# A hybrid decoder layer on one core: where the recurrence's masked matrices are transposed

## Chip, cores and metric

One core of a Trainium2 chip. The metric is the device time of one execution, in microseconds (us). The kernel before takes 2487.46 us (median of three runs, 2486.31 to 2492.12).

## The reference

One layer of a decoder is computed for a prompt of 1024 tokens and for 8 x 4 sample tokens: normalisation, one wide projection, differential attention (4 heads) beside an RWKV-7 group (8 heads of size 64), an output projection, a gated convolutional feed-forward part and a per-layer embedding. The change lies in the RWKV-7 recurrence of the prompt:

```
def _wkv_scan(s0, r, w, k, v, kk, a):
    def step(s, inp):
        r_t, w_t, k_t, v_t, kk_t, a_t = inp
        sa = jnp.einsum('bhvk,bhk->bhv', s, -kk_t)
        s = (s * w_t[:, :, None, :] + sa[..., None] * (kk_t * a_t)[:, :, None, :]
             + v_t[..., None] * k_t[:, :, None, :])
        return s, jnp.einsum('bhvk,bhk->bhv', s, r_t)
```

The kernel doesn't step through the tokens. It cuts the prompt into 16 chunks of 64 tokens. For each chunk and head it forms the chunk's transition, for which a unit triangular 64 x 64 matrix must be inverted; a short scan over the 16 chunks follows.

## The kernel before

The program is a row of blocks, each with its own instruction list for every engine; the engines wait for one another by semaphores. The block of the change is `rwkv_transitions` (L1150). Its successor is `rwkv_scan` (L1433), and then come the attention, the output projection and the rest.

`rwkv_transitions` takes the chunks two at a time, called b = 0 and b = 1, in 8 turns; the first is written out, the other seven are a loop. The 8 heads lie as 4 pairs, two heads in the 128 partitions. A tile of 128 x 512 holds, for 4 pairs, a 128 x 128 matrix that is block diagonal with two blocks of 64 x 64.

The order of the work is that of the program text on each engine. A turn is, on TensorE: products that form the triangular matrices (L1272), 32 transposes of the pair blocks (L1283), then six levels, then the last products (L1320 to L1334). The inversion goes by levels: at level n the blocks of size 2^n along the diagonal are joined to blocks of size 2^(n+1). A level has four steps for each of b = 0 and b = 1:

- mask: VectorE multiplies the current matrix (at level 0 `za` in SBUF, later the product `q0` in PSUM) by the level's mask `levbd` into `ut` (L1367); what remains lies within the blocks of size 2^(n+1), that is, up to level 4 within blocks of 32 x 32 on the diagonal
- transpose: TensorE transposes the four 128 x 128 matrices of `ut` into PSUM, `q1` (L1292)
- copy: VectorE copies `q1` to `ubd` in SBUF (L1373)
- product: TensorE multiplies with `ubd` as weights into `q0` (L1304)

On each engine both chunks' instructions of one step stand before those of the next: mask b0, mask b1, copy b0, copy b1 on VectorE; transposes of b0 and b1, products of b0 and b1 on TensorE. ScalarE copies the product to `wz` for the next level (L1391), after the next level's mask has read it. At level 0, TensorE has another group of matmuls behind the products (L1312), which needs `vs` from GpSimd (L1240). `q1` also holds, at the start of a turn, what VectorE reads into `m2` and `m4` (L1355, L1356); the semaphore `m4` keeps the transposes of level 0 from writing `q1` before. GpSimd fills `bd` for the next turn (L1225) while the levels run.

Of the kernel before, what the change touches and what calls it, by code (L numbers as in the profile page):

```python
# [904 lines left out]
NLEV = 6  # L905
# [244 lines left out]
def rwkv_transitions(kit, a, NR, BK, V, Y):  # L1150
# [14 lines left out]
    nc = kit.nc  # L1165
# [4 lines left out]
    with ExitStack() as ctx:  # L1170
# [87 lines left out]
        @block.tensor  # L1258
        def _(pe):
            pe.wait_ge(S["const_in"], 16 * len(consts))  # L1260
            mm = nc.tensor.matmul

            def turn(i, first):
                for b in range(2):
                    c = i * 2 + b
                    pe.wait_ge(S["placed"], c * 8 + 8)
                    for q, dst, freed, sem in ((0, q0, ("phi_kept", "r_kept"), "p1"), (1, q1, ("z_kept", "y_kept"), "p2")):
                        if not first:
                            for name in freed:
                                pe.wait_ge(S[name], c - 1)  # L1270
                        for p in range(NPAIR):
                            last = mm(dst[b][:, p, :], bd[:, b, q, p, :], NR[:, p, :, ds(c * C, C)],  # L1272
                                      start=True, stop=True)
                        last.then_inc(S[sem], 1)
                for r, (qa, qb) in enumerate(((0, 1), (2, 3))):
                    for b in range(2):
                        for n, (q, dst) in enumerate(((qa, q2), (qb, q3))):
                            if r == 1:
                                pe.wait_ge(S["kept"], i * 8 + 2 * b + n + 1)
                            elif not first:  # L1280
                                pe.wait_ge(S["a2v_kept" if n == 0 else "xbd"], i * 2 - 1 + b)
                            for p in range(NPAIR):
                                last = nc.tensor.transpose(dst[b][:, p, :], bd[:, b, q, p, :], ident[:])  # L1283
                            last.then_inc(S["turn"], 1)
                for lev in range(NLEV):
                    for b in range(2):
                        n = (i * NLEV + lev) * 2 + b
                        pe.wait_ge(S["ut"], n + 1)
                        if lev == 0:
                            pe.wait_ge(S["m4"], i * 2 + b + 1)  # L1290
                        for p in range(NPAIR):
                            last = nc.tensor.transpose(q1[b][:, p, :], ut[:, b, p, :], ident[:])  # L1292
                        last.then_inc(S["uturn"], 1)
                    for b in range(2):
                        n = (i * NLEV + lev) * 2 + b
                        pe.wait_ge(S["ubd"], n + 1)
                        if lev == 0:
                            pe.wait_ge(S["m3"], i * 2 + b + 1)
                            pe.wait_ge(S["adi"], i * 2 + b + 1)
                        else:  # L1300
                            pe.wait_ge(S["wz"], (i * (NLEV - 1) + lev - 1) * 2 + b + 1)
                        src, w = za if lev == 0 else wz, C if lev == NLEV - 1 else 2 * C
                        for p in range(NPAIR):
                            last = mm(q0[b][:, p, 0:w], ubd[:, b, p, :], side(src[:, b, p])[:, 0:w], start=True, stop=True)  # L1304
                        last.then_inc(S["made"], 1)
                    if lev == 0:
                        for b in range(2):
                            pe.wait_ge(S["m2"], i * 2 + b + 1)
                            pe.wait_ge(S["stacked"], i * 6 + b * 3 + 2)
                            pe.wait_ge(S["kept"], i * 8 + 8)  # L1310
                            for p in range(NPAIR):
                                last = mm(q2[b][:, p, 0:C], m2[:, b, p, :], vs[:, b, p, :], start=True, stop=True)  # L1312
                            last.then_inc(S["a2v"], 1)
                for b in range(2):
                    c = i * 2 + b
                    pe.wait_ge(S["wbd"], c + 1)
                    pe.wait_ge(S["a2v_kept"], c + 1)
                    pe.wait_ge(S["stacked"], i * 6 + b * 3 + 3)
                    for p in range(NPAIR):
                        last = mm(q3[b][:, p, :], wbd[:, b, p, :], side(na[:, b, p]), start=True, stop=True)  # L1320
                    last.then_inc(S["tx"], 1)
                for b in range(2):
                    c = i * 2 + b
                    pe.wait_ge(S["tn_kept"], c + 1)
                    for p in range(NPAIR):
                        last = mm(q0[b][:, p, :], tn[:, b, p, :], side(bm[:, b, p]), start=True, stop=True)
                    last.then_inc(S["pr"], 1)
                    pe.wait_ge(S["xst"], c + 1)
                    pe.wait_ge(S["xbd"], c + 1)
                    for p in range(NPAIR):  # L1330
                        mm(q1[b][:, p, 0:C], turned[:, b, 0, p, :], xst[:, b, p, :], start=True, stop=False)
                        mm(q1[b][:, p, 0:C], turned[:, b, 1, p, :], vs[:, b, p, :], start=False, stop=True)
                        mm(q1[b][:, p, C:P], xbd[:, b, p, :], bm[:, b, p, 1, :], start=True, stop=False)
                        last = mm(q1[b][:, p, C:P], turned[:, b, 2, p, :], m4[:, b, p, :], start=False, stop=True)  # L1334
                    last.then_inc(S["zy"], 1)
            turns(pe, turn)

        @block.vector
        def _(dve):
# [3 lines left out]
            def turn(i, first):  # L1343
                for b in range(2):
                    c = i * 2 + b
                    dve.wait_ge(S["p1"], c + 1)
                    if not first:
                        dve.wait_ge(S["zy"], c - 1)
                    tt(za[:, b, :, 1], q0[b][:, :, 0:C], pairs(below[:]), ALU.mult)\
                        .then_inc(S["adi0"], 1)  # L1350
                    tt(bm[:, b, :, 1], q0[b][:, :, C:P], pairs(incl[:]), ALU.mult).then_inc(S["m3"], 1)
                for b in range(2):
                    c = i * 2 + b
                    dve.wait_ge(S["p2"], c + 1)
                    tt(blocks(m2[:, b]), spread(q1[b][:, :, 0:C]), pairs(strict[:]), ALU.mult).then_inc(S["m2"], 1)  # L1355
                    tt(m4[:, b], q1[b][:, :, C:P], pairs(incl[:]), ALU.mult).then_inc(S["m4"], 1)  # L1356
                for lev in range(NLEV):
                    for b in range(2):
                        n = (i * NLEV + lev) * 2 + b
                        if lev == 0:  # L1360
                            dve.wait_ge(S["adi"], i * 2 + b + 1)
                        else:
                            dve.wait_ge(S["made"], n - 1)
                        if not (first and lev == 0):
                            dve.wait_ge(S["uturn"], n - 1)
                        z = za[:, b, :, 1] if lev == 0 else q0[b][:, :, C:P]
                        tt(blocks(ut[:, b]), spread(z), pairs(levbd[:, lev]), ALU.mult).then_inc(S["ut"], 1)  # L1367
                    for b in range(2):
                        n = (i * NLEV + lev) * 2 + b
                        dve.wait_ge(S["uturn"], n + 1)  # L1370
                        if not (first and lev == 0):
                            dve.wait_ge(S["made"], n - 1)
                        nc.vector.tensor_copy(ubd[:, b], q1[b][:]).then_inc(S["ubd"], 1)  # L1373
                for b in range(2):
                    c = i * 2 + b
                    dve.wait_ge(S["tx"], c + 1)
                    tt(blocks(tn[:, b]), spread(q3[b][:, :, 0:C]), pairs(pairbd[:]), ALU.mult).then_inc(S["tn_kept"], 1)
                for b in range(2):
                    c = i * 2 + b
                    here = ds(c * C, C)  # L1380
                    dve.wait_ge(S["pr"], c + 1)
                    tt(BK[:, 0, :, here], q0[b][:, :, 0:C], pairs(eye[:]), ALU.add).then_inc(S["phi_kept"], 1)
                    tt(NR[:, :, 1, here], q0[b][:, :, C:P], NR[:, :, 1, here], ALU.add).then_inc(S["r_kept"], 1)
# [1463 lines left out]
```

## Time and profile before

| what | value |
|---|---|
| median of three runs | 2487.46 us |
| the profiled execution | 2489.03 us |
| its span, first to last instruction | 2487.3 us |
| mean granted TensorE clock | 0.879 |
| TensorE busy, whole span | 2007.8 us (81%) |
| VectorE busy | 1218.6 us (49%) |
| ScalarE busy | 833.5 us (34%) |
| GpSimd busy | 450.6 us (18%) |

In the rows, PE is TensorE's matmuls, PEld its loading of weights, DVE is VectorE, ACT ScalarE, POOL GpSimd. Times count from the first instruction. A matmul's end is modelled. A row of the timeline merges instructions of one line that follow each other; what stands in brackets at its end is the idle time of the engine before it, and what ended it. A product of 32-bit matrices is two matmul instructions for each pair, so the 8 products of a step, 4 pairs of two chunks, are 16; a transpose is one.

### The profile page before, as it was taken

What the parts mean: (1) busy time and instruction counts of PE and PEld (TensorE: products, weight loads), DVE (VectorE), ACT (ScalarE), POOL (GpSimd) and SP (SyncE); (2) the same over time, 40 slices, a digit from 0 to 9 for tenths busy, and PEclk for the clock granted to TensorE, in tenths of its full rate; (3) what the DMA queues carried; (4) which work ended last, traced back from release to release, by engine and by line L of the source; (5) the groups of instructions that cost most, each with busy time, mean ns of one, the idle gap of its engine ahead of it and who ended that gap; (6) DMA issues with size and microseconds to landing.
All of it is one profiled execution on the core that took longest, in us unless ns stands there. A gap on an engine that the chain in (4) does not pass through costs nothing. (4 is left out here: it accounts for less than half of the span.)

```text
span 2487.3 us, 35830 instructions
## 1 busy us (share of the span) xinstructions
PE 2007.8 (81%) x13340; PEld 1908.8 (77%) x13340; DVE 1218.6 (49%) x1996; ACT 833.5 (34%) x1408; POOL 450.6 (18%) x606
## 2 busy tenths in 40 slices
PE   1999972439999993664565568999999998999997
PEld 1999971328889893554344568999999998999997
DVE  5001106635455523765662157656555556445475
ACT  3111114213343322553000145433333334434454
POOL 0000001443232210001960202211111110011022
PEclk8999995769999965877666689999999999999998
DMA  2222213010000005224862054111111113454443
GB/s 99 89 94 87 102 71 126 35 44 1 0 0 0 0 0 116 51 52 112 290 203 91 35 203 143 64 43 44 51 43 52 43 52 121 134 169 161 138 129 120
DMA packets 75720, 211.89 MB, mean 85 GB/s; under 512 B 11506, under 2 KB 17570, under 8 KB 75314
## 3 DMA queue, kind: packets, MB, share of 16 engines
q1 hardware_dynamic: 55986, 156.30, 20.3%
q0 software_dynamic: 8224, 31.81, 3.4%
q10 hardware_dynamic: 11392, 22.20, 2.8%
q8 instruction: 75, 1.23, 0.2%
q14 instruction: 43, 0.35, 0.0%
HBM read 179.04 MB, written 31.24 MB: 85 GB/s over the span
## 5 line engine op out<-in xcount | busy, mean ns | idle before, releaser
L2018 PE MATMUL bh_acc<-Mh,bh_wh 128*128 128x352 f32 x2016 | 659.5, 327 | 33.9 <-DVE bh_wl L2288 28.3
L2018 PE MATMUL bh_acc<-Ml,bh_wh 128*128 128x352 f32 x2016 | 652.6, 324 | 0.0
L2018 PE MATMUL bh_acc<-Mh,bh_wl 128*128 128x352 f32 x2016 | 652.5, 324 | 0.0
L2018 PEld LDWEIGHTS bh_acc<-Mh,bh_wh 128*128 128x128 f32 x2016 | 383.4, 190 | 36.7 <-DVE bh_wl L2288 29.7
L2018 PEld LDWEIGHTS bh_acc<-Ml,bh_wh 128*128 128x128 f32 x2016 | 384.3, 191 | 0.0
L2018 PEld LDWEIGHTS bh_acc<-Mh,bh_wl 128*128 128x128 f32 x2016 | 383.1, 190 | 0.0
L2288 DVE TENSOR_TENSOR bh_wl<-bh_raw,bh_wh 128x1024 fp32r<-128x1024 f32 x170 | 201.2, 1184 | 167.3 <-ACT bh_wh L2093 167.2
L403 PE MATMUL in_acc<-Hh,in_wh 128*128 128x352 f32 x624 | 202.5, 324 | 24.5 <-DVE in_wl L386 24.5
L2093 ACT ACTIVATE bh_wh<-bh_raw 128x1024 fp32r<-128x1024 f32 x170 | 173.9, 1024 | 116.4 <-PE bh_acc L2018 106.4
L403 PE MATMUL in_acc<-Hl,in_wh 128*128 128x352 f32 x624 | 201.1, 322 | 0.0
L403 PE MATMUL in_acc<-Hh,in_wl 128*128 128x352 f32 x624 | 200.9, 322 | 0.0
L2328 DVE TENSOR_TENSOR cv_u<-bh_acc,ffn_r 128x352 f32<-128x352 f32 x132 | 67.8, 514 | 191.9 <-PE bh_acc L2018 189.9
L386 DVE TENSOR_TENSOR in_wl<-in_raw,in_wh 128x1024 fp32r<-128x1024 f32 x26 | 31.8, 1225 | 252.1 <-ACT in_wh L374 252.1
L403 PEld LDWEIGHTS in_acc<-Hh,in_wh 128*128 128x128 f32 x624 | 118.0, 189 | 24.6 <-DVE in_wl L386 24.6
L532 PE MATMUL ap_sc<-ap_kh,ap_qs 128*128 128x512 f32 (+3 forms) x96 | 45.0, 470 | 93.3 <-DVE ap_kl L588 48.8
L403 PEld LDWEIGHTS in_acc<-Hl,in_wh 128*128 128x128 f32 x624 | 118.1, 189 | 0.0
L403 PEld LDWEIGHTS in_acc<-Hh,in_wl 128*128 128x128 f32 x624 | 117.8, 189 | 0.0
L288 ACT ACTIVATE in_out<-in_acc 128x1056 f32<-128x1056 f32 x26 | 27.4, 1055 | 251.9 <-PE in_acc L403 251.9
L2137 ACT ACTIVATE cv_v<-cv_u,par 128x352 f32<-128x352 f32 (+1 forms) x66 | 45.3, 686 | 175.5 <-DVE cv_u L2328 77.0
L532 PEld LDWEIGHTS ap_sc<-ap_kh,ap_qs 128*128 128x128 f32 x96 | 22.9, 239 | 99.3 <-issue 49.4
L2137 ACT ACTIVATE cv_g<-cv_u,par 128x352 f32<-128x352 f32 (+1 forms) x66 | 45.3, 686 | 119.7 <-DVE cv_u L2328 73.7
L1304 PE MATMUL rt_q<-rt_wz,rt_ubd 128*128 128x128 f32 (+1 forms) x640 | 81.5, 280 | 4.1 <-DVE rt_ubd L1373 3.4
(334 smaller groups left out, 3417.2 us busy)
## 6 DMA issues: line engine op xcount, KB each, us to landing
bh_raw<-dram_w_down SPq DMA_DIRECT2D x48, 512.0 KB, 3.7
bh_raw<-dram_w_up SPq DMA_DIRECT2D x44, 512.0 KB, 3.6
as_vp<-dram_v_pool ACTq DMA_DIRECT2D x64, 256.0 KB, 3.3
as_kT<-dram_k_pool SPq DMA_DIRECT2D x64, 256.0 KB, 4.0
dram_projT<-in_out POOLq DMA_DIRECT2D x26, 528.0 KB, 3.0
in_raw<-dram_w_in SPq DMA_DIRECT2D x26, 512.0 KB, 3.6
bh_raw<-dram_w_o SPq DMA_DIRECT2D x24, 512.0 KB, 3.7
bh_raw<-dram_w_gate SPq DMA_DIRECT2D x24, 512.0 KB, 3.6
```

Of the source, the lines that this page charges most:

```text
L288: self.nc.scalar.activation(self.out[:, b], self.acc[:, b, :, 0:self.parts[0][1]], ACT.Copy).then_inc(self.drained, 1)
L386: nc.vector.tensor_tensor(wl[:, buf], raw[:, buf], wh[:, buf].bitcast(F32), ALU.subtract).then_inc(residued, 1)
L403: last = nc.tensor.matmul(acc[:, b, n, 0:size], w[:, buf, k, :], x[:, u * kt + k, at:at + size], start=(u == 0 and k == 0 and q == 0), sto ...
L532: last = nc.tensor.matmul(sc[:, c, at:at + n], qs[:, hb, c, i * P:(i + 1) * P], k[:, hb, c, at:at + n], start=(k is kh), stop=(k is kl and ...
L1304: last = mm(q0[b][:, p, 0:w], ubd[:, b, p, :], side(src[:, b, p])[:, 0:w], start=True, stop=True)
L2018: ins = mm(out, w(k), x, start=first and k == 0 and q == 0, stop=last and k == len(xs) - 1 and q == 2)
L2093: nc.scalar.activation(whs[b][:, 0:n], raws[b][:, 0:n], ACT.Copy).then_inc(rounded, 1)
L2137: nc.scalar.activation(conv_of(m, t), u[m % 2][:, cols(t)], ACT.Identity, bias=tap("cb", m), scale=tap("cw0", m)).then_inc(tap0, 1)
L2288: nc.vector.tensor_tensor(wls[b][:, 0:n], raws[b][:, 0:n], whs[b][:, 0:n].bitcast(F32), ALU.subtract).then_inc(residued, 1)
L2328: ins = nc.vector.tensor_tensor(z[:, 2 + at:2 + at + w], src[:, 0:w], R1[:, at:at + w], ALU.mult)
```

## The change

At levels 0 to 4 VectorE transposes `ut` straight into `ubd`, both in SBUF, by its block transpose, one instruction of 128 x 512 for each chunk. It turns every block of 32 x 32 in its place, which is the transpose of the whole where all that isn't zero lies in 32 x 32 blocks on the diagonal. Level 5, whose blocks are 64 x 64, keeps the transpose on TensorE and the copy. The waits follow: the product waits for `ubd` as before, a mask waits for the transpose that read its buffer, and TensorE's wait for `m4` moves to level 5.

```diff
                 for lev in range(NLEV):
-                    for b in range(2):
+                    for b in range(2 if lev == NLEV - 1 else 0):
                         n = (i * NLEV + lev) * 2 + b
                         pe.wait_ge(S["ut"], n + 1)
-                        if lev == 0:
-                            pe.wait_ge(S["m4"], i * 2 + b + 1)
+                        pe.wait_ge(S["m4"], i * 2 + b + 1)
                         for p in range(NPAIR):
                             last = nc.tensor.transpose(q1[b][:, p, :], ut[:, b, p, :], ident[:])
                         last.then_inc(S["uturn"], 1)
...
-                        if not (first and lev == 0):
-                            dve.wait_ge(S["uturn"], n - 1)
+                        if lev:
+                            dve.wait_ge(S["ubd"], n - 1)
+                        elif not first:
+                            dve.wait_ge(S["uturn"], i * 2 - 1 + b)
                         z = za[:, b, :, 1] if lev == 0 else q0[b][:, :, C:P]
                         tt(blocks(ut[:, b]), spread(z), pairs(levbd[:, lev]), ALU.mult).then_inc(S["ut"], 1)
                     for b in range(2):
                         n = (i * NLEV + lev) * 2 + b
-                        dve.wait_ge(S["uturn"], n + 1)
                         if not (first and lev == 0):
                             dve.wait_ge(S["made"], n - 1)
-                        nc.vector.tensor_copy(ubd[:, b], q1[b][:]).then_inc(S["ubd"], 1)
+                        if lev < NLEV - 1:
+                            dve.wait_ge(S["ut"], n + 1)
+                            nc.vector.transpose(ubd[:, b].rearrange("p a c -> p (a c)"),
+                                                ut[:, b].rearrange("p a c -> p (a c)")).then_inc(S["ubd"], 1)
+                        else:
+                            dve.wait_ge(S["uturn"], i * 2 + b + 1)
+                            nc.vector.tensor_copy(ubd[:, b], q1[b][:]).then_inc(S["ubd"], 1)
```

## Rows read from the trace of the kernel before

**Rows 1.** Chain of waits, its earliest piece: start us, us, what.

```profile
1446.52 1.06 ACT bh_wh L2093
```

**Rows 2.** Stretches, all engines: PE, PEld, DVE, ACT, POOL busy; clock; DMA share; GB/s.

```profile
640.00:680.00 40.00, 38.11 (x315) 35.12 (x314) 22.27 (x38) 14.99 (x32) 12.01 (x24) 1.00 0.00 0
```

**Rows 3.** Timeline, start of two turns: start us, us, engine, line, operation, tiles.

```profile
640.25 0.42 DVE L1349 TENSOR_TENSOR rt_za<-rt_q,rt_below 128x256 f32<-128x256 f32 x1 [3.69 <-PE rt_q L1272]
...
681.12 0.42 DVE L1349 TENSOR_TENSOR rt_za<-rt_q,rt_below 128x256 f32<-128x256 f32 x1 [3.69 <-PE rt_q L1272]
```

**Rows 4.** Timeline, one steady level (level 3) of that turn.

```profile
657.32 0.69 DVE L1367 TENSOR_TENSOR rt_ut<-rt_q,rt_levbd 128x512 f32<-128x512 f32 x1 [0.49 <-PE rt_q L1304]
658.04 0.60 ACT L1391 ACTIVATE rt_wz<-rt_q 128x512 f32<-128x512 f32 x1 [2.03 <-DVE rt_ut L1367]
...
658.07 0.66 PE L1292 MATMUL rt_q<-rt_ident,rt_ut 128*128 128x128 f32 x4
658.21 0.69 DVE L1367 TENSOR_TENSOR rt_ut<-rt_q,rt_levbd 128x512 f32<-128x512 f32 x1 [0.20 <-PE rt_q L1304]
658.82 0.68 DVE L1373 COPY rt_ubd<-rt_q 128x512 f32<-128x512 f32 x1
...
658.96 0.66 PE L1292 MATMUL rt_q<-rt_ident,rt_ut 128*128 128x128 f32 x4 [0.23 <-DVE rt_ut L1367]
...
659.64 2.05 PE L1304 MATMUL rt_q<-rt_wz,rt_ubd 128*128 128x128 f32 x16
...
660.83 0.69 DVE L1367 TENSOR_TENSOR rt_ut<-rt_q,rt_levbd 128x512 f32<-128x512 f32 x1 [0.49 <-PE rt_q L1304]
```

**Rows 5.** Timeline, levels 0 and 1 of the same turn.

```profile
642.64 3.66 PE L1283 MATMUL rt_q<-rt_ident,rt_bd 128*128 128x128 f32 x32
...
644.48 1.44 DVE L1367 TENSOR_TENSOR rt_ut<-rt_za,rt_levbd 128x512 f32<-128x512 f32 x2
...
646.13 1.04 PE L1292 MATMUL rt_q<-rt_ident,rt_ut 128*128 128x128 f32 x8
...
646.77 1.29 DVE L1373 COPY rt_ubd<-rt_q 128x512 f32<-128x512 f32 x2 [0.85 <-PE rt_q L1292]
...
647.51 2.05 PE L1304 MATMUL rt_q<-rt_za,rt_ubd 128*128 128x128 f32 x16 [0.35 <-DVE rt_ubd L1373]
648.05 0.73 POOL L1240 TENSOR_TENSOR rt_vs<-rt_turned 128x256 f32<-128x256 f32 x1
...
649.40 1.90 PE L1312 MATMUL rt_q<-rt_vs,rt_m 128*128 128x64 f32 x16
...
651.13 1.05 PE L1292 MATMUL rt_q<-rt_ident,rt_ut 128*128 128x128 f32 x8
...
651.78 1.29 DVE L1373 COPY rt_ubd<-rt_q 128x512 f32<-128x512 f32 x2 [1.49 <-PE rt_q L1292]
...
652.61 2.05 PE L1304 MATMUL rt_q<-rt_wz,rt_ubd 128*128 128x128 f32 x16 [0.43 <-DVE rt_ubd L1373]
```

**Rows 6.** Groups of VectorE by shape: busy us, mean ns, idle before.

```profile
L2288 DVE TENSOR_TENSOR bh_wl<-bh_raw,bh_wh 128x1024 fp32r<-128x1024 f32 x146 | 178.2, 1221 | 122.8 <-ACT bh_wh L2093 122.7
L1373 DVE COPY rt_ubd<-rt_q 128x512 f32<-128x512 f32 x96 | 64.5, 686 | 23.5 <-PE rt_q L1292 22.3
...
L614 DVE SCALAR_TENSOR_TENSOR ap_wgt<-ap_pexp,ap_small,ap_wgt 128x512 f32<-128x512 f32 x4 | 3.0, 752 | 0.4
...
L610 DVE TENSOR_SCALAR ap_wgt<-ap_pexp,ap_small 128x512 f32<-128x512 f32 x4 | 1.9, 476 | 0.0
```

**Rows 7.** Stretches in the attention: PE busy (count), clock, DMA share, GB/s.

```profile
1003.70:1007.10 3.40, 1.50 (x12) 1.00 0.00 0
...
1007.00:1008.00 1.00, 1.00 (x6) 0.58 0.00 0
...
1010.60:1017.40 6.80, 3.38 (x31) 1.00 0.00 0
```

**Rows 8.** A stretch in the scan, columns as in rows 2.

```profile
890.00:900.00 10.00, 10.00 (x49) 10.00 (x48) 3.22 (x8) 2.48 (x6) 2.20 (x6) 0.50 0.01 2
```

## Prediction

> **What bounds the kernel now.** I read the chain of waits first. Its earliest piece stands at 1446.52 us [rows 1], so it says nothing of the transitions, which run from about 555 to 885 us. The stretches come next: in 640 to 680 us TensorE is busy 38.11 of 40 us, VectorE 22.27, ScalarE 14.99, with the granted clock at 1.00 and no DMA [rows 2]. That looks like a stage bound by TensorE, but these times include the modelled tails of matmuls, so only the timeline tells who waits for whom. The two starts of L1349, one turn apart, give a turn of 681.12 - 640.25 = 40.87 us [rows 3], and there are eight turns: 16 chunks by two, and L1373's 96 copies are 8 x 6 levels x 2 chunks [rows 6].
>
> A steady level first [rows 4]. b0 and b1 are the two chunks. The masking of b0 (ut, L1367) starts at 657.32 and that of b1 at 658.21, since b1's waits for its own product. TensorE transposes b0 from 658.07 for 0.66 us, while VectorE masks b1. The copy of b0 (L1373) starts at 658.82, 0.61 after b1's masking started, which is the pitch of 512-column operations on VectorE standing behind one another; it has no idle time before it. So b0's transposes are hidden behind the masking of b1. The product (L1304) starts at 659.64, 0.14 after that copy ends, and the next masking at 660.83, another 1.19 later. A level is 660.83 - 657.32 = 3.51 us, bound by a ring through VectorE and TensorE: masking of b1 0.61, copy 0.68 and 0.14, product to next masking 1.19, masking of b0 to that of b1 0.89.
>
> The first two levels of a turn are different [rows 5]. In level 0 VectorE has masked both chunks by 645.92, but TensorE still works through the 32 transposes of the pair blocks (L1283, 642.64 for 3.66 us). It reaches the transposes of ut only at 646.13, and the copies start at 646.77 after 0.85 us of idle time. In level 1 it is worse: TensorE has 16 matmuls of L1312 queued ahead (649.40 for 1.90), the transposes start at 651.13, and VectorE waits 1.49 us until 651.78. Here the transposes on TensorE, which executes in order, end last.
>
> **The change part by part.** Removed at levels 0 to 4: 8 transposes on TensorE per level (1.04 to 1.05 us where they stand together, two lots of 0.66 in a steady level), their semaphores, and 2 PSUM copies per level. Added: 2 VectorE transposes, SBUF to SBUF, 128x512, in the place of the copies, in the same order (mask b0, mask b1, transpose b0, transpose b1). VectorE has the same number of instructions. Its wait for TensorE becomes a wait for its own masking, which has ended when the transpose's turn comes: b0's masking ends 0.20 us before b1's starts, and b1's ends while b0 is transposed. Nothing else is queued behind it that was not behind the copy. Level 5 and the rest of the turn stay.
>
> *The duration T of a VectorE transpose.* No row shows one. The copy that it replaces takes 0.686 mean, but reads PSUM. The nearest SBUF rows of 512 columns are 0.476 (L610, one tensor input) and 0.752 (L614, two) [rows 6]; level 0's two maskings, from SBUF, take 1.44 together. Below, 0.476. Above, twice the elements: 1.22 (L2288, 1024 columns), if 4-byte elements go through in two passes. I take 0.71, between the copy and L614, since a transpose is one pass with some filling ahead of the first output.
>
> *Steady levels (2 to 4).* The ring is unchanged except for T in place of 0.68, so a level costs T - 0.68 = 0.03 more and the three of them lose 0.09 us. TensorE's transposes were hidden there, and taking them out gives nothing back.
>
> *Level 0.* The transpose of b0 starts at VectorE's pitch, about 645.85, ends at 646.56, and the product starts 0.05 later (the gap after the copy there), at 646.61 in place of 647.51: 0.90 earlier. TensorE has finished L1283 by 646.30.
>
> *Level 1.* Two things may end last. TensorE: L1312 follows the start of the product by 649.40 - 647.51 = 1.89, and the next instruction came 651.13 - 649.40 = 1.73 after that, so it is free at 646.61 + 3.62 = 650.23. What L1312 needs from GpSimd for b1 (the vs of 648.05, 0.73 long [rows 5]) is there at 648.78, before b1's half at about 649.4. VectorE: 646.61 + 1.19 + 0.89 + 0.61 + 0.71 + 0.14 = 650.15. So TensorE by a hair: the product starts at 650.23 in place of 652.61, 2.38 earlier (0.90 of it from level 0).
>
> *Sum.* 2.38 - 0.09 = 2.29 us per turn, 8 turns, 18.3 us. The turns follow one another through the same rings, and the scan starts after the stage, with next to no DMA beside it [rows 2, 8], so all of it should arrive at the end. The profiled execution took 2489.03 (span 2487.3, and 1.7 around it): 2470.7. The median of the three runs is 1.57 lower, so I forecast 2469.
>
> In general the gain of a turn is the smaller of 3.09 - T and 3.88 - 2T, less 3(T - 0.68). At 0.476 that is 3.2 us, 25.8 in all, 2462.
>
> *A figure of the Trainium skill weighed against this.* The rows put the gain where TensorE's transposes are late, in levels 0 and 1, and at nothing where they are hidden [rows 4, 5]. The Trainium skill, page "VectorE: DVE Perf Modes", section "The three transpose paths", lists 390 ns for a 128x128 bf16 transpose on TensorE and 311 ns on VectorE. By that difference, as an estimate, the 8 x 5 x 8 = 320 tiles would save 0.079 each wherever they stand, 25 us and 2462; that is rival D. I go by the rows.
>
> **The rivals.**
>
> *A: the transpose is slow.* At T over 0.96 also b1's product waits, since its transpose then ends more than 0.89 after b0's. The five levels then lose T - 0.96 each on top, and the gain of a turn is about 10.7 - 10T: nothing at T = 1.07, and at 1.22 a loss of 1.5 per turn, 12 us, 2499. For it: 4-byte data, and no row of this operation. Against it: the rows of 512 columns lie between 0.476 and 0.752 [rows 6]. The Trainium skill, "Vector Engine (DVE) Microarchitecture Reference", section 3.8, has the transpose array sustain one element per cycle and lane, which speaks against two passes; no row here shows it.
>
> *B: the clock falls, the case on the other side of the forecast.* The place is the bursts of levels 1 to 4. TensorE is left with 2.05 us of matmuls per 3.51 us, where it had two lots of transposes of 0.66 besides [rows 4]. If that drops the clock from 2.4 to 1.2 GHz, the four bursts of levels 2 to 5 take 2.05 longer each, 8.2 per turn against 2.3 gained: 47 us, 2534. It decides from 1.1 slow bursts per turn on. For it: in the scan TensorE's records fill 10 of 10 us and the clock stays at 0.50 [rows 8], and in 3.40 us from 1003.70 TensorE was busy 1.50 and the clock fell right after [rows 7]. Against it: in 6.80 us from 1010.60 it was busy 3.38, and the clock stayed at 1.00 [rows 7]; the levels after the change stand nearer to this one, though for longer. The Trainium skill, "TensorE: Matmul & The Clock Gate", part 4, says that transposes on TensorE don't count as its being busy; by that rule these levels hold the clock on the matmuls alone already, and taking the transposes out changes nothing. No run here separates the two.
>
> *C: the transposes at level 0 or 1 are hidden anyway* by something that I overlook, for instance GpSimd's adds, which use SBUF while the transposes run (the last vs at 648.05 [rows 5]), or a wait in front of L1312. Then only about half the gain remains: 1.2 per turn, 2478.
>
> *D: VectorE's transpose is the quicker one in every level*, as the rate of L610 would make it: with T at 0.476 a steady level loses 0.20 too, 3.2 us per turn, 2462 as above. No row of a transpose bears it out.
>
> **How the numbers follow.** Forecast (T between 0.6 and 0.8, 2.0 to 2.7 per turn) 0.73; its own range is 2464 to 2474, with some two microseconds on either side for the spread of the runs (2486.31 to 2492.12). A 0.10, B 0.07, C 0.05, D 0.05. The measurement tells about 0.3%, 7.5 us. Faster: forecast, C, D and some of neither, 0.82. Same: A with T between 0.9 and 1.1, and a part of C, 0.07. Slower: A at 1.2, and B, 0.11. The range 2460 to 2481 takes in C and D and leaves out A's long end and B.
>
> **What would show it.** Steady levels still 3.5 us apart, with the transpose 0.61 behind the second masking and TensorE idle some 1.3 us between bursts; the idle times of 0.85 and 1.49 before VectorE's second pair gone in levels 0 and 1; L1312 followed at once by level 1's product; a turn of about 38.6 us; clock 1.00 throughout. The forecast is wrong if a VectorE transpose takes over 0.9, if the product waits for ScalarE's wz (it ends at 658.64 for b0, 0.9 ahead of need [rows 4]), or if the turn shrinks by steady levels.

## The result, and the profile after

| | before | after |
|---|---|---|
| median of the runs | 2487.42 us (4 runs, 2486.31 to 2492.12) | 2471.34 us (4 runs, 2467.08 to 2474.39) |
| ratio after to before, 95% | | 0.9931 (0.9911 to 0.9951) |
| profiled execution, its span | 2489.03, 2487.3 | 2467.08, 2464.9 |
| turn, start of `za` to the next one | 40.87 | 38.52 |
| stage: first `za` to the scan's first memset | 329.00 | 309.95 |

The kernel is faster by 0.5 to 0.9%, which is 12 to 22 us; 2469 was forecast, and the median is 2.3 above that. The lines have moved: masks are now L1368, the VectorE transpose L1375, the copy of level 5 L1379, the product L1303, TensorE's own transposes L1291, and the group behind level 0 L1311.

The turn comes from the timeline of VectorE (start us, busy us, engine, line, operation, tiles), two starts of `za` in the kernel after. They answer to [rows 3]:

```profile
637.53 0.42 DVE L1348 TENSOR_TENSOR rt_za<-rt_q,rt_below 128x256 f32<-128x256 f32 x1 [3.69 <-PE rt_q L1272]
...
676.05 0.42 DVE L1348 TENSOR_TENSOR rt_za<-rt_q,rt_below 128x256 f32<-128x256 f32 x1 [3.69 <-PE rt_q L1272]
```

The stage's two ends, from the same view:

```profile
559.64 0.42 DVE L1348 TENSOR_TENSOR rt_za<-rt_q,rt_below 128x256 f32<-128x256 f32 x1 [17.09 <-PE rt_q L1272]
...
869.59 0.27 DVE L1520 MEMSET rn_states<- 128x256 f32 x1 [4.64 <-PEq L71]
```

The stretch of [rows 2], by engine, in the kernel after (PE, PEld, DVE, ACT and POOL busy, clock, DMA share, GB/s):

```profile
640.00:680.00 40.00, 34.89 (x296) 33.23 (x295) 23.39 (x42) 16.48 (x36) 12.60 (x26) 1.00 0.00 0
```

TensorE is less busy, the others a little more, since 40 us now hold more of a turn. The clock stays at 1.00, which is 2.4 GHz.

The price that no row of before had, the VectorE transpose, from the groups of VectorE's work by shape (count, then busy us and mean ns, then idle time before):

```profile
L1375 DVE STREAM_TRANSPOSE rt_ubd<-rt_ut 128x512 f32<-128x512 f32 x80 | 51.8, 684 | 0.0
...
L1379 DVE COPY rt_ubd<-rt_q 128x512 f32<-128x512 f32 x16 | 11.1, 692 | 1.6 <-PE rt_q L1291 1.6
```

684 ns, as much as the copy that it replaces (686 in [rows 6], 692 for the ones left at level 5), and VectorE never sat idle in front of one.

Levels 0 and 1 of that turn, from the timeline of all engines; they answer to [rows 5]:

```profile
639.92 3.66 PE L1283 MATMUL rt_q<-rt_ident,rt_bd 128*128 128x128 f32 x32
...
641.76 1.44 DVE L1368 TENSOR_TENSOR rt_ut<-rt_za,rt_levbd 128x512 f32<-128x512 f32 x2
643.12 1.29 DVE L1375 STREAM_TRANSPOSE rt_ubd<-rt_ut 128x512 f32<-128x512 f32 x2
...
643.88 2.05 PE L1303 MATMUL rt_q<-rt_za,rt_ubd 128*128 128x128 f32 x16 [0.30 <-DVE rt_ubd L1375]
...
645.76 1.90 PE L1311 MATMUL rt_q<-rt_vs,rt_m 128*128 128x64 f32 x16
...
646.57 1.29 DVE L1375 STREAM_TRANSPOSE rt_ubd<-rt_ut 128x512 f32<-128x512 f32 x2
...
647.50 2.00 PE L1303 MATMUL rt_q<-rt_wz,rt_ubd 128*128 128x128 f32 x16
```

The idle times of 0.85 and 1.49 in front of VectorE's second pair are gone. From the first mask to level 1's product it takes 647.50 - 641.76 = 5.74; before it took 652.61 - 644.48 = 8.13 [rows 5]. Level 1's product follows L1311 with no idle time: TensorE is the one that ends last there.

A steady level, from the same view; it answers to [rows 4]:

```profile
652.18 0.69 DVE L1368 TENSOR_TENSOR rt_ut<-rt_q,rt_levbd 128x512 f32<-128x512 f32 x1 [0.74 <-PE rt_q L1303]
...
652.90 0.60 ACT L1397 ACTIVATE rt_wz<-rt_q 128x512 f32<-128x512 f32 x1 [2.04 <-DVE rt_ut L1368]
653.07 0.69 DVE L1368 TENSOR_TENSOR rt_ut<-rt_q,rt_levbd 128x512 f32<-128x512 f32 x1 [0.20 <-PE rt_q L1303]
...
653.68 1.29 DVE L1375 STREAM_TRANSPOSE rt_ubd<-rt_ut 128x512 f32<-128x512 f32 x2
...
654.52 2.05 PE L1303 MATMUL rt_q<-rt_wz,rt_ubd 128*128 128x128 f32 x16 [1.49 <-ACT rt_wz L1397]
655.72 0.69 DVE L1368 TENSOR_TENSOR rt_ut<-rt_q,rt_levbd 128x512 f32<-128x512 f32 x1 [0.74 <-PE rt_q L1303]
```

A level takes 655.72 - 652.18 = 3.54, where it took 3.51. The releaser that the product's row names, ScalarE's `wz`, is not the one: for b0 it had ended at 652.90 + 0.60 = 653.50, while the transpose of b0, started at 653.68, ends 0.68 later, 0.16 before the product. Where a row names an engine that had long been done, look for the other input of the waiting instruction.

### The profile page after: what moved, and what is told of

Read it like the earlier page. It is cut to its first block and busy times, and to the rows that moved or that the text cites. A ratio compares the mean times of both kernels' runs of the same rounds, so it can differ in the third digit from the quotient of the medians.

```text
span 2464.9 us, 35120 instructions
## 1 busy us (share of the span) xinstructions
PE 1957.7 (79%) x13020; PEld 1868.9 (76%) x13020; DVE 1215.9 (49%) x1996; ACT 833.1 (34%) x1408; POOL 450.4 (18%) x606
## 5 line engine op out<-in xcount | busy, mean ns | idle before, releaser
L532 PE MATMUL ap_sc<-ap_kh,ap_qs 128*128 128x512 f32 (+3 forms) x96 | 43.1, 449 | 98.1 <-DVE ap_kl L588 49.5
L1303 PE MATMUL rt_q<-rt_wz,rt_ubd 128*128 128x128 f32 (+1 forms) x640 | 81.1, 280 | 35.8 <-ACT rt_wz L1397 31.3
L1303 PEld LDWEIGHTS rt_q<-rt_wz,rt_ubd 128*128 128x128 f32 x640 | 74.5, 192 | 42.1 <-ACT rt_wz L1397 37.1
```

The costliest lines, as they stand in the source:

```text
L532: last = nc.tensor.matmul(sc[:, c, at:at + n], qs[:, hb, c, i * P:(i + 1) * P], k[:, hb, c, at:at + n], start=(k is kh), stop=(k is kl and ...
```

## Experiments

Seven kernels ran. In the table the time is the median (one run where no spread stands), the ratio is to the kernel before in the same study (medians 2486.48 for experiments 1 to 4, 2486.83 for 5 to 7), and `turn`, `level` (a steady one, start to start) and `stage` are from each one's trace. Experiments 1 to 4 ran on one chip, 5 to 7 on another. Line numbers shift by a few from one experiment to the next; the tiles tell which step a row is.

| | us | ratio, 95% | turn | level | stage |
|---|---|---|---|---|---|
| before | 2487.42 | 1 | 40.87 | 3.51 | 329.00 |
| after | 2471.34 | 0.9931 (0.9911 to 0.9951) | 38.52 | 3.54 | 309.95 |
| 1: levels 0, 1 only | 2475.36 (2470.67 to 2478.84) | 0.9952 (0.9935 to 0.9969) | 38.44 | 3.51 | 309.55 |
| 2: levels 2 to 4 only | 2494.08 (2491.2 to 2501.33) | 1.003 (1.0007 to 1.0052) | 40.95 | 3.54 | 329.69 |
| 3: other order | 2457.49 (2456.23 to 2459.01) | 0.9886 (0.987 to 0.9903) | 36.74 | 2.77 | 296.41 |
| 4: transposes twice | 2524.6 | | 44.24 to 46.94 | 4.41 to 5.9 | 366.83 |
| 5: 4, with TensorE transposes | 2505.02 | | 43.01 | 4.41 | 345.57 |
| 6: 4, with TensorE products | 2502.62 | | 43.01 | 4.41 | 345.81 |
| 7: 3, L1311 spread | 2448.05 (2446.52 to 2452.93) | 0.984 (0.9815 to 0.9864) | 35.77 | 2.76 | 288.47 |

### 1 and 2: which levels give the gain

Experiment 1 leaves levels 2 to 4 to TensorE and the copy, experiment 2 leaves levels 0 and 1 to them. The waits follow (not shown).

```diff
-                    for b in range(2 if lev == NLEV - 1 else 0):
+                    for b in range(2 if lev in PEL else 0):
...
-                        if lev < NLEV - 1:
+                        if lev not in PEL:
                             dve.wait_ge(S["ut"], n + 1)
# experiment 1: PEL = (2, 3, 4, 5); experiment 2: PEL = (0, 1, 5)
```

> VectorE's transpose at levels 0 and 1 alone; levels 2 to 5 transpose on TensorE and copy, as before. Theory (the gain comes where TensorE's in-order queue delayed the transposes, in levels 0 and 1): the turn falls from 40.88 to about 38.5 us, as with the whole change (38.52), steady levels at 3.51, some 2468 to 2472. Rival (each tile taken off TensorE is worth the same, wherever it stands): two fifths of the gain of 2.36 per turn, a turn of about 39.9 us, some 2480.

> The other part: VectorE's transpose at levels 2, 3 and 4 alone. Theory: TensorE's transposes are hidden there behind the second masking, so nothing is gained: a turn of 40.9 to 41.0 us, steady levels 3.53, time within 0.2% of before. Rival: three fifths of the gain, a turn of about 39.5 us, some 2476.

Two turns' starts of experiment 1, from VectorE's timeline, then of experiment 2:

```profile
641.26 0.42 DVE L1350 TENSOR_TENSOR rt_za<-rt_q,rt_below 128x256 f32<-128x256 f32 x1 [3.69 <-PE rt_q L1273]
...
679.70 0.42 DVE L1350 TENSOR_TENSOR rt_za<-rt_q,rt_below 128x256 f32<-128x256 f32 x1 [3.69 <-PE rt_q L1273]
```

```profile
639.16 0.42 DVE L1350 TENSOR_TENSOR rt_za<-rt_q,rt_below 128x256 f32<-128x256 f32 x1 [3.69 <-PE rt_q L1273]
...
680.11 0.42 DVE L1350 TENSOR_TENSOR rt_za<-rt_q,rt_below 128x256 f32<-128x256 f32 x1 [3.69 <-PE rt_q L1273]
```

Levels 0 and 1 alone give the whole gain and a little more (40.87 - 38.44 = 2.43 a turn, against 2.35 with all five levels), and the three steady levels alone lose 0.08. Both turns are as the theory had them; an edge in every level, which asked for turns of 39.9 and 39.5, is refuted by both.

The times of the whole program are not as the theory had them. Experiment 1 was to take 2468 to 2472 and took 2475.36; experiment 2 was to stay within 0.2% of before and is slower by 0.1 to 0.5%. Experiment 1 gained 11 us where its stage gained 329.00 - 309.55 = 19.45, and experiment 2 lost 7.6 where its stage lost 0.7. The other kernels lean the same way: for the one after the change and for experiments 1, 2, 3 and 7, the median lies 1.8 to 8.3 us above what the median before and the change of the stage together would give. What lies outside the stage, which no experiment touched, also differs between the profiled executions: the stage begins between 556.09 and 563.31 us, and from its end to the end of the span it takes 1595.3 to 1603.3. For experiment 1 these were 563.31 and 1602.4, where before had 557.48 and 1600.8: 5.8 and 1.6 later, the 7.4 between its span's gain of 12.0 and its stage's gain. For experiment 2 the profiled execution, the fastest of the seven, doesn't show where the 7.6 of the median lie. The cause of these differences stays open; they don't follow the levels, since levels 2 to 4 on VectorE go with a median 4.0 us lower between experiment 1 and the whole change, and 7.6 higher between before and experiment 2. So the gain of this change is best read from the stage, and the median carries some microseconds that the stage doesn't explain.

### 3: the order on VectorE

With the transpose on VectorE, its order need not be that of the kernel before. Here b0 is transposed before b1 is masked, at levels 0 to 4. The bodies of the two loops over b, unchanged, become functions that are not shown: `mask`, and `swap`, which transposes or, at level 5, copies.

```diff
+                    order = (mask, 0), (mask, 1), (swap, 0), (swap, 1)
+                    if lev < NLEV - 1:
+                        order = (mask, 0), (swap, 0), (mask, 1), (swap, 1)
+                    for step, b in order:
+                        step(lev, b)
```

> The whole change with VectorE's order at levels 0 to 4 made mask b0, transpose b0, mask b1, transpose b1 (before: both masks, then both transposes). Theory (a steady level is a ring in which b0's transpose stands behind the masking of b1): the ring opens, and VectorE's own work with the wait for its mask's end (0.69 and some 0.15, then 0.61, for each chunk) sets a level of about 2.9 us in place of 3.53. From level 0's product to level 1's stays 3.6, set by TensorE. A turn of about 36.3 us, 2.2 less than with the change, some 2453. Rival (the ring is set by product, ScalarE's copy wz and semaphores, and VectorE's order doesn't matter): 38.5 us. Rival (the wait for its own mask costs VectorE more than is won): levels of 3.5 us or more.

Experiment 3, timeline of all engines, a steady level:

```profile
647.31 0.69 DVE L1367 TENSOR_TENSOR rt_ut<-rt_q,rt_levbd 128x512 f32<-128x512 f32 x1
...
648.03 0.71 DVE L1375 STREAM_TRANSPOSE rt_ubd<-rt_ut 128x512 f32<-128x512 f32 x1
648.67 0.65 DVE L1367 TENSOR_TENSOR rt_ut<-rt_q,rt_levbd 128x512 f32<-128x512 f32 x1
...
648.89 1.15 PE L1303 MATMUL rt_q<-rt_wz,rt_ubd 128*128 128x128 f32 x8 [0.30 <-DVE rt_ubd L1375]
649.36 0.71 DVE L1375 STREAM_TRANSPOSE rt_ubd<-rt_ut 128x512 f32<-128x512 f32 x1
...
650.08 0.69 DVE L1367 TENSOR_TENSOR rt_ut<-rt_q,rt_levbd 128x512 f32<-128x512 f32 x1
```

A level is 2.77, a little under the 2.9 that was expected. VectorE has no idle time in front of any of its rows, and its four operations start 0.72, 0.64, 0.69 and 0.72 apart. Yet it is not VectorE's own pace that closes the level, as the expectation had it: the last distance, from b1's transpose to the next mask of b0, is longer than the 0.64 from b0's transpose to b1's mask, and that next mask stands 650.08 - 648.89 = 1.19 behind b0's product, the same distance as in a steady level before [rows 4]. So b0's own ring ends last: mask to transpose 0.72, transpose to product 0.86, product to mask 1.19, 2.77 in all. With 0.64 in place of the last 0.72, VectorE alone would need 2.69, an estimate that no run tests. A transpose follows its own mask by 0.69 to 0.72, where a transpose behind the other chunk's mask stands 0.61 after it (653.07 to 653.68 above): waiting for the operation just before costs some 0.1, less than was allowed for.

Level 0 fell short. Its rows in experiment 3:

```profile
639.20 1.15 PE L1303 MATMUL rt_q<-rt_za,rt_ubd 128*128 128x128 f32 x8
...
640.69 1.13 PE L1303 MATMUL rt_q<-rt_za,rt_ubd 128*128 128x128 f32 x8 [0.35 <-DVE rt_ubd L1375]
...
641.66 1.90 PE L1311 MATMUL rt_q<-rt_vs,rt_m 128*128 128x64 f32 x16
...
643.39 2.00 PE L1303 MATMUL rt_q<-rt_wz,rt_ubd 128*128 128x128 f32 x16
```

b1's product comes 1.49 after b0's, the 16 matmuls of L1311 stand behind it on TensorE, and so they start 2.46 after b0's product, where it was 1.88. Level 1's product waits for those 16, not for its `ubd`: 4.19 from product to product where 3.6 was expected. That makes the turn 36.74 in place of 36.3. The kernel is faster than the one after the change all the same, by 2471.34 - 2457.49 = 13.9 us, and by 309.95 - 296.41 = 13.5 in the stage.

### 4: a transpose of double length

Each VectorE transpose runs twice, the first time into `spare`, a new tile that nothing reads.

```diff
+                            nc.vector.transpose(spare[:, b].rearrange("p a c -> p (a c)"),
+                                                ut[:, b].rearrange("p a c -> p (a c)"))
                             nc.vector.transpose(ubd[:, b].rearrange("p a c -> p (a c)"),
                                                 ut[:, b].rearrange("p a c -> p (a c)")).then_inc(S["ubd"], 1)
```

> The whole change with each of VectorE's transposes at levels 0 to 4 made twice, the first time into a tile that nobody reads. Theory (the transpose is on the ring, and b1's product follows b1's transpose once this ends over 0.89 us after b0's): each level loses 0.61 for the added transpose ahead of b0's product and 0.33 since the products then stand 1.22 apart in place of 0.89; five levels, 4.7 per turn: 43.2 us, a steady level near 4.5, some 2508. Rival (VectorE has idle time in the level that takes it): 38.5 us.

The turns are 1 to 4 us longer than the longer ring alone was to make them. TensorE's timeline in experiment 4, products of three levels one after the other, shows the first 4.41 apart and the next 5.33:

```profile
662.49 2.33 PE L1303 MATMUL rt_q<-rt_wz,rt_ubd 128*128 128x128 f32 x16 [0.35 <-DVE rt_ubd L1377]
...
666.90 3.25 PE L1303 MATMUL rt_q<-rt_wz,rt_ubd 128*128 128x128 f32 x16 [2.08 <-DVE rt_ubd L1377]
...
672.23 3.78 PE L1303 MATMUL rt_q<-rt_wz,rt_ubd 128*128 128x128 f32 x16 [2.08 <-DVE rt_ubd L1377]
```

and the stretches of the same kernel show what goes with it (length, TensorE busy, granted clock, DMA share, GB/s):

```profile
660.00:664.00 4.00, 3.63 (x31) 1.00 0.00 0
664.00:668.00 4.00, 1.92 (x15) 0.94 0.00 0
668.00:672.00 4.00, 2.14 (x11) 0.50 0.00 0
672.00:676.00 4.00, 3.77 (x16) 0.50 0.00 0
676.00:680.00 4.00, 1.92 (x10) 0.50 0.00 0
680.00:684.00 4.00, 3.62 (x26) 0.85 0.00 0
```

TensorE works 2.33 and idles 2.08 in each level, and inside the levels the clock drops from 2.4 to 1.2 GHz. The same products then take 3.25 to 3.78 in place of 2.33. The kernel after idles 1.49 per level and holds the clock. The expectation had only the longer ring: 43.2 and 2508.

### 5 and 6: does a transpose on TensorE hold the clock?

Both are experiment 4 with extra work on TensorE behind the products of levels 1 to 3, the stretch in which it would idle: 8 transposes of the identity in experiment 5, 4 products of identity by identity (8 matmul instructions) in experiment 6. Nothing reads their results.

```diff
+                    if lev in (1, 2, 3):
...
+                        for b in range(2):
+                            for p in range(NPAIR):
+                                nc.tensor.transpose(q1[b][:, p, :], ident[:], ident[:])
# experiment 6, in place of the last three lines:
+                        for p in range(NPAIR):
+                            mm(q1[p % 2][:, p, :], ident[:], ident[:], start=True, stop=True)
```

> The kernel with each transpose on VectorE made twice, and on TensorE, behind the products of levels 1, 2 and 3, eight transposes of the identity that nobody reads (0.9 us in an idle time of 2.08). Theory (in the run without them the turn was 45.8 in place of 43.2 us because the clock fell to 0.50 in the longer idle times, and TensorE's transposes count as activity, as they did before the change): the clock stays at 1.00, steady levels of 4.41, a turn of 43.1 us. The Trainium skill's rule (transposes on TensorE do not count as its being busy; page TensorE: Matmul & The Clock Gate, part 4): the clock falls as without them, and the turn stays near 45.8 us. Rival (the fall has nothing to do with the idle times): 45.8 us as well, here and with matmuls in their place.

> The same with four products of the identity with itself (eight matmul instructions of 128 columns) in place of the eight transposes. Theory, and the rule of the page as well: the clock stays at 1.00, steady levels of 4.41, a turn of 43.1 us. Rival (idle times don't matter): the clock falls and the turn is near 45.8 us.

Experiment 5, TensorE's timeline:

```profile
655.45 2.33 PE L1303 MATMUL rt_q<-rt_wz,rt_ubd 128*128 128x128 f32 x16 [0.35 <-DVE rt_ubd L1383]
657.62 1.04 PE L1310 MATMUL rt_q<-rt_ident 128*128 128x128 f32 x8
659.86 2.33 PE L1303 MATMUL rt_q<-rt_wz,rt_ubd 128*128 128x128 f32 x16 [1.21 <-DVE rt_ubd L1383]
```

and the stretch of 620 to 680 us in experiments 4, 5 and 6, in that order:

```profile
620.00:680.00 60.00, 47.04 (x321) 0.81 0.00 1
```

```profile
620.00:680.00 60.00, 51.50 (x414) 1.00 0.00 0
```

```profile
620.00:680.00 60.00, 51.60 (x415) 1.00 0.00 0
```

Added work made the program faster than experiment 4, by 19.6 and 22.0 us between single runs on two chips, on which the kernel before agrees to 0.4 us (2486.48 and 2486.83): the idle time per level falls from 2.08 to 1.21, the clock stays at 1.00, every level takes 4.41 and a turn 43.01, in both alike. In the stage the two gain 21.3 and 21.0. So here TensorE's transposes hold the clock as well as products do. That contradicts the sentence of the Trainium skill that the prediction weighed under rival B ("TensorE: Matmul & The Clock Gate", part 4), that transposes don't count as TensorE's being busy; for this case the measurement decides. The trace lists these transposes as MATMUL like the products, so whether they run in the mode that the page speaks of is not shown.

Experiment 5 also gives the true price of a ring lengthened by a second transpose: 43.01 - 38.52 = 4.49 a turn; the rest of experiment 4, 366.83 - 345.57 = 21.3 over the stage, is the clock.

### 7: L1311 out of the way

Experiment 3 with L1311's 16 matmuls spread, four behind each product of levels 1 to 4, and ScalarE's copies of their result moved from level 1 to levels 3 and 5.

```diff
-                    if lev == 0:
-                        for b in range(2):
+                    if 1 <= lev <= 4:
+                        b, part = divmod(lev - 1, 2)
...
-                            for p in range(NPAIR):
+                        for p in (2 * part, 2 * part + 1):
```

> VectorE's order interleaved as in the run before, and L1311's 16 matmuls taken from behind level 0's products and put in fours behind the products of levels 1 to 4; ScalarE's two copies of their result follow at levels 3 and 5. Theory (from level 0's product to level 1's TensorE's queue sets 4.19 us, steady levels are set by VectorE at 2.77): the first falls to about 2.8, the four levels lose at most 0.2 each, and the turn goes from 36.73 to between 35.3 and 36.1 us, some 2445 to 2452. Rival (TensorE has no room left, the matmuls cost as much where they go): 36.7 us.

Experiment 7, timeline, b0's products of levels 0 and 1, then a steady level from b1's product of level 2 to that of level 3:

```profile
641.48 1.15 PE L1303 MATMUL rt_q<-rt_za,rt_ubd 128*128 128x128 f32 x8
...
644.24 1.15 PE L1303 MATMUL rt_q<-rt_wz,rt_ubd 128*128 128x128 f32 x8
...
648.46 1.15 PE L1303 MATMUL rt_q<-rt_wz,rt_ubd 128*128 128x128 f32 x8 [0.27 <-DVE rt_ubd L1377]
...
649.45 0.56 PE L1312 MATMUL rt_q<-rt_vs,rt_m 128*128 128x64 f32 x4
...
649.84 1.12 PE L1303 MATMUL rt_q<-rt_wz,rt_ubd 128*128 128x128 f32 x8
...
651.22 1.15 PE L1303 MATMUL rt_q<-rt_wz,rt_ubd 128*128 128x128 f32 x8 [0.25 <-DVE rt_ubd L1377]
```

From level 0's product to level 1's it now takes 644.24 - 641.48 = 2.76, where it took 4.19 (expected: 2.8). The four matmuls (L1312 here) fit behind b1's product and in front of b0's next one, which then has no idle time before it, and the level stays at 651.22 - 648.46 = 2.76. The turn falls by another 0.97 to 35.77, so 0.46 of the 1.43 won in front of level 1 is lost behind it. This version beats both kernels: it is 1.4 to 1.9% faster than the one before, and 2471.34 - 2448.05 = 23.3 us under the one after.

## Why the prediction was right, point by point

- **Level 0, 0.90.** From the first mask to the product: 643.88 - 641.76 = 2.12, before 647.51 - 644.48 = 3.03 [rows 5]. The gain is 0.91.
- **Level 1, 2.38 in all.** Measured 8.13 - 5.74 = 2.39. That TensorE would end last there by a hair holds too: L1311 follows the product by 1.88 and holds TensorE for 1.74 more, while b0's transpose, started at 646.57, was done at 647.25, which by 0.16 as in a steady level would have let the product start at 647.41, 0.09 earlier than it did.
- **Steady levels, -0.03 each.** 3.54 against 3.51, with the two lots of TensorE's transposes (0.66 each [rows 4]) taken out for nothing. Experiment 2 shows the same with these levels alone.
- **T, taken as 0.71.** Measured 0.684, nearest to the copy's 0.686; the terms hang on it by a few hundredths. That it is one pass with some filling, the reason given, no run here tests.
- **The idle time of TensorE.** "Some 1.3 us between bursts" was too small by its own figures, 3.51 - 2.05 = 1.46; measured 1.49. No term and no rival hung on it.
- **The sum, 2.29 a turn.** Measured 40.87 - 38.52 = 2.35; over the stage 19.05 against 18.3. The profiled execution gained 22.0, since the rest of the program ran some 3 us shorter in it; the medians differ by 16.1. "All of it should arrive at the end" can therefore only be said to some microseconds. That the median came within 2.3 us of the forecast is in part luck: experiment 1, with as good a stage, came out 4.0 us higher.
- **Rival A** (a slow transpose) did not occur, but experiment 4 tests its working. With the second one behind it at a pitch of 0.61, T is 0.61 + 0.68 = 1.29, and "10.7 - 10T" gives a loss of 2.2 a turn, 43.1; experiments 5 and 6 measured 43.01. Its price was wrong all the same: it left out that the longer idle time would also take the clock, and experiment 4, without extra work, came out some 20 us dearer. In that kernel A and B came together.
- **Rival B** (the clock falls) did not occur at 1.49 idle per level; its mechanism exists, as experiment 4 shows. The prediction left open whether TensorE's transposes had been holding the clock; experiments 5 and 6 say that such transposes can, and the kernel after that its levels don't need them.
- **Rivals C and D.** The gain at levels 0 and 1, 0.91 and 2.39 in all, is not the half that C had, and D's T of 0.476 was not found. Both fall with experiments 1 and 2 besides: the transposes of levels 0 and 1 were not hidden, those of levels 2 to 4 were. The 390 and 311 ns of the Trainium skill's "VectorE: DVE Perf Modes" ("The three transpose paths") led D to 25 us from every level; what counted was where the transposes were late, and by how much.

What the prediction did not see is that the change makes another order possible. Before, a copy of b0 ahead of b1's masking would have waited for TensorE, which has b0's transposes done only at 658.07 + 0.66 = 658.73, 0.52 after b1's masking starts [rows 4]; no run tests that order in the kernel before. With the transpose on VectorE it waits for the mask just done, and that order is worth 13.9 us more.

## What to carry to other kernels

Taking work off an engine gains where that work ends last, and only there: find, level by level, the idle time that it ended, add these up, and leave the rest of the removed work at nothing. When a step changes its engine, ask again for the order of the steps on the engine that receives it, since the old order may have covered a wait that is gone. And a longer wait for TensorE can cost its clock as well, so price the two together.

## What the runs showed of the hardware

- A VectorE transpose of 128 x 512 in f32, SBUF to SBUF, takes 684 ns (660 to 703 over 80), as long as a copy of the same shape out of PSUM (692), and follows the mask in front of it by 0.61 where it needn't wait for that one, by 0.69 to 0.72 where it does (steady levels of experiment 3).
- With 2.33 us of products and 2.08 of idle time in turn, the granted clock fell from 1.00 to 0.50 within three levels (experiment 4); with 2.05 of products and 1.49 of idle time, as in the kernel after, it stayed at 1.00. Eight transposes of 128 x 128 on TensorE in each gap, 1.04 us, held it as well as eight matmul instructions of 1.06 did (experiments 5 and 6). What decides between these two cases was not measured.
